# Projection matmuls cut into three pieces of 256 columns instead of 256 and 512

## What is computed

```
def trunk(x, mem, p):
    for i in range(DEPTH):                      # DEPTH = 2
        x = x + hybrid_mixer(rmsnorm(x, ...), p, i)      # u @ w_in, Hyena + SSD, y @ w_out
        x = x + memory_cross_attention(rmsnorm(x, ...), rmsnorm(mem, ...), w_q, w_kv, w_o)
        hdn = rmsnorm(x, ...) @ p["w_up"][i]             # 1024 x 4096
        x = x + jnp.square(jax.nn.relu(hdn)) @ p["w_down"][i]
    return rmsnorm(x, p["norm_final"])
```

## Time and profile before

| | |
|---|---|
| median of 3 runs | 2409.13 us (2407.44 to 2411.49) |
| span of the profiled execution | 2407.6 us |
| TensorE (PE) busy | 2384.1 us, 99%, 12908 matmuls |
| weight loads (PEld) busy | 2068.8 us, 86%, 12908 |
| VectorE / ScalarE / GpSimd busy | 54% / 46% / 16% |
| mean DMA rate | 116 GB/s |

### The profile page before, as it was taken

How to read it: one execution, slowest core, us unless ns; L and a number is a source line. 1 busy time by engine, 2 the same in 40 slices (tenths; PEclk the granted TensorE clock), 3 DMA queues, 4 the chain that set the end, 5 groups by cost and what they waited for, 6 DMA issues and landing times.

```text
span 2407.6 us, 33120 instructions
## 1 busy us (share of the span) xinstructions
PE 2384.1 (99%) x12908; PEld 2068.8 (86%) x12908; DVE 1311.3 (54%) x2070; ACT 1119.5 (46%) x2167; POOL 395.9 (16%) x456
## 2 busy tenths in 40 slices
PE   8999999999999999999999999999999999999997
PEld 6888668898888999989888885788988889999996
DVE  8877585366335452626378776734753265344353
ACT  5544435455445453536445435355454454444352
POOL 1111002210112121211111110022001121212121
PEclk9999999999999999999999999999999999999998
DMA  5545326852355565555555553278315555656563
GB/s 160 109 99 105 88 97 138 174 127 62 75 123 120 126 134 124 125 128 120 114 115 110 101 119 88 62 180 175 92 44 109 123 123 121 132 125 127 118 132 101
DMA packets 111863, 279.48 MB, mean 116 GB/s; under 512 B 12694, under 2 KB 12950, under 8 KB 111716
## 3 DMA queue, kind: packets, MB, share of 16 engines
q0 software_dynamic: 65088, 118.52, 29.5%
q1 hardware_dynamic: 46628, 158.93, 22.1%
HBM read 274.25 MB, written 3.15 MB: 115 GB/s over the span
## 4 chain that ended last, share of the span: by engine, by line
PE 98%; DVE 1%; DMA 1%; ACT 0%; issue 0%; DVEq 0%; POOL 0%; SPq 0%; ACTq 0%
PE G L1110 55%; PE G L1609 2%; PE M L1609 2%; PE M L1610 2%; PE G L1610 2%; PE M L1611 2%; PE G L1611 2%; PE M L1329 2%; PE G L1540 2%; PE M L1075 2%; PE M L1073 2%; PE M L1074 2%; PE M L1110 1%; PE M L1062 1%; PE G L1342 1%; PE M L1397 1%
## 5 line engine op out<-in xcount | busy, mean ns | idle before, releaser
L535 POOL DMA_DIRECT2D wlo<-wstream x376 | 330.0, 881 | 1538.0 <-ACT wlo L568 1300.6
L568 ACT ACTIVATE wlo<-raw 128x512 fp32r<-128x512 f32 x344 | 216.4, 629 | 653.2 <-PE G L1110 571.1
L1110 PE MATMUL G<-B_lo,whi 128*128 128x256 f32 x1248 | 423.1, 339 | 0.0
L1110 PE MATMUL G<-B_hi,whi 128*128 128x256 f32 x1248 | 395.5, 339 | 0.0
L1110 PE MATMUL G<-A_lo,whi 128*128 128x256 f32 x1120 | 376.6, 341 | 0.0
L1110 PE MATMUL G<-A_hi,whi 128*128 128x256 f32 x1120 | 358.8, 344 | 10.5 <-DVE A_lo L1704 9.0
L1675 DVE TENSOR_TENSOR X<-X,G 128x768 f32<-128x768 f32 x92 | 87.7, 953 | 437.5 <-PE G L1110 341.6
L1110 PE MATMUL G<-B_hi,wlo 128*128 128x256 f32 x1248 | 317.1, 335 | 0.0
L1110 PE MATMUL G<-A_hi,wlo 128*128 128x256 f32 x1120 | 284.9, 335 | 0.0
L1110 PEld LDWEIGHTS G<-B_hi,wlo 128*128 128x128 f32 x1248 | 234.4, 188 | 56.6
L1110 PEld LDWEIGHTS G<-B_lo,whi 128*128 128x128 f32 x1248 | 235.5, 189 | 26.3
(11 more groups left out here) (444 smaller groups left out, 4377.3 us busy)
## 6 DMA issues: line engine op xcount, KB each, us to landing
raw<-wstream SPq DMA_DIRECT2D x228, 512.0 KB, 4.0
wlo<-wstream POOLq DMA_DIRECT2D x376, 256.0 KB, 5.3
w_low<-wstream POOLq DMA_DIRECT2D x72, 256.0 KB, 4.2
raw_b<-wstream SPq DMA_DIRECT2D x24, 512.0 KB, 6.8
ring<-dft SPq DMA_DIRECT2D x12, 512.0 KB, 3.3
mraw<-memT SPq DMA_DIRECT2D x16, 256.0 KB, 3.3
X<-xT SPq DMA_DIRECT2D x8, 384.0 KB, 6.8
win<-dft SPq DMA_DIRECT2D x6, 512.0 KB, 6.2
```

The lines of the kernel that those rows point to most:

```text
L535: pool.dma_start(low, wstream[stream(L, c)][:, part], accum_op=ALU.add).then_inc(lo_in[c % 2][h], 16)
L568: act.activation(wlo[:, s, part], raw[:, s, part], ACT.Copy, scale=-1.0).then_inc(neg_done, 1)
L1110: last = mm(out, w, p[:, k, a:b], start=(k == 0 and w is w_hi and p is parts[0]), stop=(k == KT - 1 and (w is w_lo and only is None or onl ...
```

## The change

Every stream tile is multiplied in three pieces of 256 columns, every memory tile in two. The first two pieces of a stream tile open a bank each; the third adds into the bank that the second has opened, without a `start` of its own. `skip_group_check` only silences a check at build time.

```diff
+THIRDS, MEM_HALVES = ((0, 256), (256, 512), (512, 768)), ((0, 256), (256, 512))
...
-            def tile(..., cols=SEGS, ks=(0, KT), ...):
+            def tile(..., cols=THIRDS, ks=(0, KT), ...):
+                first = 256 if cols is THIRDS else 512
...
                     for w, parts in passes:
                         for a, b in cols:
-                            out = PS[tp][:, 256 + a:256 + b] if len(cols) == 2 else PS[tp][:, 512:1024]
+                            out = PS[tp][:, first + a:first + b]
                             for p in parts:
-                                last = mm(out, w, p[:, k, a:b], start=(k == 0 and w is w_hi and p is parts[0]),
-                                          stop=(k == KT - 1 and (w is w_lo and only is None or only == "low")))
+                                opens = k == 0 and w is w_hi and p is parts[0] and (first + a) % 512 in (0, 256 - a)
+                                last = mm(out, w, p[:, k, a:b], start=opens,
+                                          stop=(k == KT - 1 and (w is w_lo and only is None or only == "low")),
+                                          skip_group_check=True)
...
-                    tile(L * CH + (C_OUT + m), m % 2, t, OUT_BANKS[m], xa, ready, hook, SEGS, ks, hook_at, m == 2,
+                    tile(L * CH + (C_OUT + m), m % 2, t, OUT_BANKS[m], xa, ready, hook, THIRDS, ks, hook_at, m == 2,
...
-                    tile(L * CH + C_K + j, j % 2, L * TILES + T_K + j, j % 2, xm, None, hook, ((0, M2),),
+                    tile(L * CH + C_K + j, j % 2, L * TILES + T_K + j, j % 2, xm, None, hook, MEM_HALVES,
```

More of the change, by code:

```diff
@@ L1083, in half_in, with tile @@
                     pe.wait_ge(lo_in[s][h], c * 8 - 8 * s)
-            def tile(c, slot, t, tp, src, ready=None, hook=None, cols=SEGS, ks=(0, KT), hook_at=None, aside=False, only=None):
+            def tile(c, slot, t, tp, src, ready=None, hook=None, cols=THIRDS, ks=(0, KT), hook_at=None, aside=False, only=None):
+                first = 256 if cols is THIRDS else 512
                 if ks[0] == 0:
```

## The result

The changed kernel takes 2446.16 us (2444.32 to 2446.48, four runs) against 2410.31 for the kernel before in the same comparison: a ratio of 1.0147, 95% interval 1.0135 to 1.0158. It is 36 us slower, where 9.8 were forecast and a range that ended at 2427.

What follows compares the result with a forecast made beforehand. PE was taken to bound the kernel, the time being the sum of its matmuls. Splits added 8.9 us in stream k-steps and 0.9 for keys: 2407.6 + 9.8 = 2417.4, plus 1.5 for the median, 2418.9 us; range 2406 to 2427.

Steps and rivals of the forecast that it cites:

- What bounds the kernel: Whole kernel: PE is busy 99% of 2407.6 us, so the time is the sum of its matmuls' cost.
- The counts: Stream tiles and keys: 1216 k-steps go from six to nine pairs, keys add 384; +4032 pairs, 12908 to 16940.
- What one split costs: Each 512 cut into two 256s on PE: +2.4 ns a split, +7.3 ns a k-step, +9.8 us with the keys.
- the upper end: Dearest reading of the split on PE, from the step-size projection: 4032 x 4.3 ns, +17.3 us.
- Does the load keep up?: Weight loads on PE: a load needs 112 ns, 117.5 is 5 ns above that, so nothing is added.
- The first rival: Split matmuls on PE: a column costs the same in any cut; 2407.5 us, up to 2413.9; chance 0.25.
- Rival B: Weight loads set PE's pace, starting later and later: nine 256s take 1080 ns, 2448.9 us; chance 0.08.
- Rival C: Short pieces on PE are faster: a k-step at 1.02 us, -36.7 us, 2372.4 us; chance 0.07.
- Does the sequencer keep up?: PE's instruction issue: 59 ns per instruction needed, 111 ns a pair seen against 117.5 needed; nothing added.
- The sign: Skill's rule for PE matmuls, N / 2.4 + 2.5 ns: its constant speaks against the change, 10.1 us.

Runs made afterwards that it cites:

- e3: Changed kernel with each of the three stream pieces 288 columns wide instead of 256, overlapping a neighbour; 2583.1 us.
- e9: Changed kernel with each of the three stream pieces 320 columns wide instead of 256; 2734.99 us.
- e10: Changed kernel with projection matmuls loading 112 of the 128 weight columns from the second block of k on; 2389.88 us.
- e11: Kernel before, with loops over column ranges and activation parts exchanged (256, 512, 256, 512); 2405.17 us against 2409.7, ratio 0.9982.

## Why the prediction was wrong, by its own steps

- *What bounds the kernel.* Right. The time is the sum of the gaps on PE: 1216 x 29.7 ns and 1.9 us for the keys give the difference of the spans to 1.2 us.
- *The counts*, 1216 k-steps, +4032 pairs: right, 16940 on the page.
- *What one split costs.* This is the term that failed: +2.4 ns was put for a split, and it measured 9.9 on average in the stream tiles (6.4 for the low pass, 11.5 each for the high one) and 4.9 in the keys. It took 117.5 ns for a 256 from the step-size projection, and the new stream shows 120.0. The working named the difference, 32 weight columns against 128, and passed over it; with 32 columns the very same tiles go at 118.1 ns, which accounts for most of it there, though the keys at 114.2 ns show that the agreement is not a rule. Even the upper end, 17.3 us, was built on the same row, so the range had no bound that looked at full loads.
- *Does the load keep up?* Costed at nothing, with "5 ns" of cover. The 112 ns of the earlier trace rows were measured beside matmuls of one column and not beside a full stream. Rows of the right shape were on the table: the k-step of the earlier trace rows has its gap of 0.12 us at a 256 with full loads, twice. At 120 ns each, nine are 1080, and that was the answer. The text called the 0.12 a rounding, and for one of the two it was: by the starts in the trace the medians of these gaps before are 117 and 120 ns. So the rows did not prove 120, but they allowed it, and the range should have held it.
- *The first rival, a column costs the same in any cut.* Wrong. The 384s fit it only because a single width can't tell 0.4553 ns a column from 0.439 and 6 ns a pair; e3 and e9 needed two widths to part them.
- *Rival B*: its price for the k-step, nine at 120 ns, was right, its mechanism was not shown, and to that extent the near hit of 2448.9 is luck; for the keys it had 3.6 us where 1.9 were paid. Loads start on time. As bookkeeping, the line of e3, e9 and the earlier trace rows puts 18.1 of the 29.7 ns on three more pairs at 6.0 ns each, and 11.6 on what the 256s of stream tiles pay over that line; it is no mechanism, since the keys, the order and the width all move the price.
- *Rival C.* Did not come with full loads. Its thought that a gap moves with what runs beside it was sound: with 112 weight columns it went to 113.3 ns.
- *Does the sequencer keep up?* Right: e10 has the same instructions at 114.6 ns.
- *The Trainium skill*, "TensorE: Matmul & The Clock Gate", section "Back-to-back issue gap", has 2.5 ns on top of N / 2.4, and says that this is the gap of an isolated matmul, not of a stream of pairs; the prediction left that condition out. The sign was right and the size was not: 6 ns a pair and 0.439 ns a column in the even runs of 288 to 384 columns here, where its figures are 2.5 and 0.417.

What stays open is why a 256 with a full load takes 120.0 ns in these tiles. With the weights' width the gap of an even run goes up and down between 113 and 120 ns, with the order of pieces it moves by about 1 ns a pair, with the tile (keys or stream) by 1.3 ns, within a block of half the rows it stays, and the same code runs at two levels in two layers. That reads like a rhythm between load and stream that falls into one of several patterns, but no run here shows the mechanism. No run moved the operands in SBUF or the output to another bank with all else kept.

## What to carry to other kernels

Where TensorE is the bound, count pairs of load and matmul, not columns alone, and do not take one price for all of them: splitting a 512 into two 256s cost 5 to 12 ns here, never nothing. How much depended on the place, the width of the weights and the order, so the price has to be taken in the very tile that is changed. When a price is taken from another place in the trace, it must match in every operand's shape, and where it doesn't, the range has to be built from a row that does. Two widths are needed to part a price per column from a price per instruction; one width fits either.

## What the hardware showed that was not expected

With half the rows (e5), TensorE's granted clock fell to its low level, 1.2 GHz of 2.4, for long stretches, although the profile has PE busy without a gap. Two stretches (us, PE busy, PEld, DVE, ACT, POOL, PEclk, DMA share, GB/s):

```profile
700.00:740.00 40.00, 40.00 (x324) 38.92 (x323) 11.37 (x12) 16.63 (x26) 7.76 (x9) 1.00 0.58 116
850.00:890.00 40.00, 40.00 (x181) 38.66 (x181) 8.13 (x9) 11.54 (x19) 4.31 (x5) 0.50 0.35 73
```

181 matmuls in 40 us against 324. The mean clock of the run was 0.907, against 0.996 before. The run is 297 us longer than the kernel after; the changes between 64 and 128 rows are 56 us of that by the estimate above, which leaves some 240 us for the clock. No trace kept here of a kernel with full rows shows a mean clock below 0.995, not even with a quarter of the weight columns (e6, 0.996).

Two more: at the high clock a change of the rows in use cost about 183 ns each time (e5), and one and the same stretch of code kept 1040 ns a k-step in one layer and 1060 in the other (e11).
